# Gate matmuls of the second block's experts as fp32r halves, with GpSimd multiplying the low ones, and the choices of experts in another order

## The reference, cut to what matters

```python
def peer_ffn(h, peer_wq, peer_k1, peer_k2, peer_u, peer_v):
    q = (ht @ peer_wq).reshape(T, 8, 256)
    s1, s2 = q[..., :128] . peer_k1, q[..., 128:] . peer_k2        # T x 8 x 128 each
    v1, i1 = lax.top_k(s1, 16);  v2, i2 = lax.top_k(s2, 16)
    sc, pos = lax.top_k(v1[..., :, None] + v2[..., None, :], 16)   # best 16 of 256 pairs
    experts = i1[pos // 16] * 128 + i2[pos % 16]                   # T x 128 of 16384
    gates = softmax(sc)
    a = gelu(peer_u[experts] . h) * gates
    out = a @ peer_v[experts]
```

## Time and profile before

| what | value |
|---|---|
| time, three runs | median 2980.7 us (2978.4 to 2987.61) |
| the profiled execution | 2978.2 us |
| its span, first to last instruction | 2976.5 us |
| TensorE busy | 2824.8 us, 95% |
| VectorE busy | 2235.7 us, 75% |
| ScalarE busy | 1481.7 us, 50% |
| GpSimd busy | 582.0 us, 20% |
| mean granted clock of TensorE | 0.98 of full |

### The profile page before, as it was taken

How to read it: one execution, slowest core, us unless ns; L and a number is a source line. 1 busy time by engine, 2 the same in 40 slices (tenths; PEclk the granted TensorE clock), 3 DMA queues, 4 the chain that set the end, 5 groups by cost and what they waited for, 6 DMA issues and landing times.

```text
span 2976.5 us, 37320 instructions
## 1 busy us (share of the span) xinstructions
PE 2824.8 (95%) x13639; PEld 2359.7 (79%) x13639; DVE 2235.7 (75%) x3019; ACT 1481.7 (50%) x1990; POOL 582.0 (20%) x460
## 2 busy tenths in 40 slices
PE   5989987999999989999999999899999999999998
PEld 3666756888888857776777789899999998888887
DVE  6465546888888863696964599999777658888886
ACT  3433235888888843544552333555665633333332
POOL 0200111111111100000000000233333324444442
PEclk7999998999999999999999999999999999999999
DMA  7544635999999833232334324688998999999995
GB/s 305 171 160 146 212 137 205 368 372 367 363 360 352 324 140 128 86 114 89 117 106 149 114 86 142 236 293 308 322 319 310 326 337 358 368 364 357 362 371 174
DMA packets 201771, 737.90 MB, mean 248 GB/s; under 512 B 24432, under 2 KB 77808, under 8 KB 145008
## 3 DMA queue, kind: packets, MB, share of 16 engines
q1 hardware_dynamic: 124656, 497.12, 46.3%
q0 software_dynamic: 55056, 170.87, 16.7%
q10 hardware_dynamic: 21872, 67.48, 5.9%
HBM read 666.61 MB, written 93.91 MB: 256 GB/s over the span
## 4 chain that ended last, share of the span: by engine, by line
PE 64%; DVE 13%; issue 4%; ACT 2%; DMA 1%; ACTq 0%; DVEq 0%; SPq 0%; POOLq 0%
PE PS L544 55%; DVE wlo L1891 3%; PE PS L1145 2%; PE PS L1011 1%; PE PS L1023 1%; DVE hf L2700 1%; ACT whi L1221 1%; PE PS L850 1%; DVE oh L2674 1%; DVE hf L2688 1%; ACT HH L1861 1%; DVE cand L2640 1%; DVE cand L2642 1%; PE PS L1002 1%; DVE sS L2727 0%
## 5 line engine op out<-in xcount | busy, mean ns | idle before, releaser
L1891 DVE TENSOR_TENSOR wlo<-raw,whi 128x2048 fp32r<-128x2048 f32 x392 | 894.2, 2289 | 311.9 <-ACT whi L1221 270.9
L1221 ACT ACTIVATE whi<-raw 128x2048 fp32r<-128x2048 f32 x392 | 750.7, 1916 | 371.5 <-PE PS L544 317.3
L544 PE MATMUL PS<-HH,whi 128*128 128x512 f32 (+1 forms) x2056 | 787.8, 383 | 20.1 <-ACT HH L1257 10.1
L544 PE MATMUL PS<-HH,wlo 128*128 128x512 f32 (+1 forms) x2056 | 750.6, 365 | 0.0
L544 PE MATMUL PS<-HL,whi 128*128 128x512 f32 (+1 forms) x2056 | 750.3, 365 | 0.0
L544 PEld LDWEIGHTS PS<-HH,whi 128*128 128x128 f32 x2056 | 390.5, 190 | 78.1 <-issue 20.4
L544 PEld LDWEIGHTS PS<-HL,whi 128*128 128x128 f32 x2056 | 390.6, 190 | 46.6 <-issue 7.7
L544 PEld LDWEIGHTS PS<-HH,wlo 128*128 128x128 f32 x2056 | 389.3, 189 | 43.3
L544 PE MATMUL PS<-whi,HH 128*128 128x512 f32 (+1 forms) x896 | 350.6, 391 | 11.1 <-DVE HL L2730 5.8
L544 PE MATMUL PS<-whi,HL 128*128 128x512 f32 (+1 forms) x896 | 346.8, 387 | 0.0
L544 PE MATMUL PS<-wlo,HH 128*128 128x512 f32 (+1 forms) x896 | 346.8, 387 | 0.0
(11 more groups left out here) (434 smaller groups left out, 3891.9 us busy)
## 6 DMA issues: line engine op xcount, KB each, us to landing
raw<-in_moe_dram SPq DMA_DIRECT2D x192, 1024.0 KB, 7.2
raw<-in_u_units_dram SPq DMA_DIRECT2D x64, 1024.0 KB
raw<-in_v_units_dram SPq DMA_DIRECT2D x64, 1024.0 KB
raw<-in_w_in_dram SPq DMA_DIRECT2D x44, 1024.0 KB
raw<-in_w_ada_dram SPq DMA_DIRECT2D x24, 1024.0 KB, 20.1
acts_dram<-sS ACTq DMA_DIRECT2D x64, 384.0 KB
gates_dram<-XT ACTq DMA_DIRECT2D x24, 1024.0 KB
sS<-acts_dram SPq DMA_DIRECT2D x42, 384.0 KB
```

The costliest lines, as they stand in the source:

```text
L544: ins = t.matmul(dst, a, b, start=(first and n == 0), stop=(last and n == 2))
L1221: a.inc(a.e.activation(m.whi[p % HRING][:, :, :], m.raw[RAW_SLOT[load_of(p)]][:, :, :], ACT.Copy), "hi", p)
L1891: v.inc(v.e.tensor_tensor(m.wlo[h][:, :, :], m.raw[RAW_SLOT[load_of(p)]][:, :, :], m.whi[h][:, :, :].bitcast(F32), ALU.subtract), "lo_v", p)
```

## The change

Tile 0 is chosen first, so that gathered rows can start in chunk 13. A tile's exponential moves three chunks behind the end of its choice and behind that chunk's gate steps on ScalarE, and its sum, reciprocal and product (the share) four chunks behind, on VectorE. A gate matmul in fp32 becomes two in fp32r: one-hots are fp32r, the gates are split into a high part (ScalarE's copy into eT as fp32r) and the rest (`glow`, one VectorE instruction for a tile), ScalarE weights with the high part, and GpSimd multiplies the same one-hots with the low part into free corners of HH and HL (`gate_low`). ScalarE's weighting comes one step later, behind GpSimd. The planner counts 650 instead of 1100 for TensorE's gate step and may put two into one chunk, which it does in 16; by its arithmetic gate steps lie in chunks 33 to 119, tile 1 is chosen in chunks 12 to 28, tile 2 in 28 to 50 and tile 3 in 51 to 75. Semaphores follow.

```diff
-CHOICE_ORDER = (1, 0, 2, 3)
-CHOICE_NS = (1500, 4600, 4600, 2000, 3400, 3400, 3400, 3400, 800, 700)
+CHOICE_ORDER = (0, 1, 2, 3)
+CHOICE_NS = (1500, 4600, 4600, 2000, 3400, 3400, 3400, 3400, 800)
+EXP_AFTER, SHARE_AFTER, SHARE_NS = 3, 4, 700
...
-        row = ([], [], [])
+        row = ([], [], [], [i for i in chosen if n == chosen[i] + EXP_AFTER], [i for i in shared if n == shared[i]])
...
-            tensor += 1100
+            tensor += 650
...
-                self.oh = sb(s2, "oh", [128, 4, 2, 4, 128])
+                self.glow = sb(s2, "glow", [128, 2, 128])
+                self.oh = sb(s2, "oh", [128, 4, 2, 4, 128], F32R)
...
+def gate_low(m, n):
+    return (m.HH, m.HL)[n % 4 // 2][:, 4 * (n % 2):4 * (n % 2) + 4, 0:TD]
...
         for k in range(4):
-            ins = t.matmul(m.PS[:, 5 + n % 3, 128 * k:128 * k + 128], m.oh[:, n % 4, 0, k, :],
-                           m.oh[:, n % 4, 1, k, :], start=True, stop=True)
+            out = m.PS[:, 5 + n % 3, 128 * k:128 * k + 128]
+            t.matmul(out, m.oh[:, n % 4, 0, k, :], m.oh[:, n % 4, 1, k, :], start=True, stop=False)
+            ins = t.matmul(out, gate_low(m, n)[:, k, :], m.oh[:, n % 4, 1, k, :], start=False, stop=True)
...
-        a.inc(s.activation(m.eT[k % 2][:, 0:384], m.PS[:, 4, 0:384], ACT.Copy), "eT", i)
-    n = step - 3
+        a.inc(s.activation(m.eT[k % 2][:, 256:384].bitcast(F32R), m.PS[:, 4, 256:384], ACT.Copy), "eT_part", i)
+        a.inc(s.activation(m.eT[k % 2][:, 0:256], m.PS[:, 4, 0:256], ACT.Copy), "eT", i)
+    n = step - 4
     if 0 <= n < N_GATE:
         k, q = divmod(n, 32)
-        a.wait_ge("onehot", n)
+        a.wait_ge("lowered", n)
...
-        for step in PEER[n][0]:
-            act_choice_step(a, m, step)
         for step in PEER[n][1]:
             act_gate_step(a, m, step)
+        for i in PEER[n][3]:
+            act_choice_exp(a, m, i)
...
+        if q == 0:
+            if k > 1:
+                v.wait_ge("lowered", 32 * (k - 1) - 1)
+            v.inc(v.e.tensor_tensor(m.glow[:, k % 2, :], m.PS[:, 4, 256:384], eT[:, 256:384], ALU.subtract), "glow",
+                  TD // 128 + k)
+            v.own()
...
+        for i in PEER[n][4]:
+            dve_choice_share(v, m, i)
...
+def pool_gate_step(g, m, step):
+    n = step - 3
+    if 0 <= n < N_GATE:
+        k, q = divmod(n, 32)
+        g.wait_ge("glow", TD // 128 + k)
+        g.wait_ge("onehot", n)
+        g.inc(g.e.tensor_tensor(gate_low(m, n), m.oh[:, n % 4, 0, :, :].bitcast(F32),
+                                bass.AP(m.glow, 128 * (k % 2) + 4 * q, [[256, 128], [1, 4], [0, 128]]), ALU.mult),
+              "lowered", n)
...
     for n in range(128):
+        for step in PEER[n][1]:
+            pool_gate_step(g, m, step)
         for step in PEER[n][2]:
             pool_rows(g, m, step)
```

More of the change, by code:

```diff
@@ L174, in peer_schedule @@
 def peer_schedule():
-    up, chosen, a, b, c = [], {}, 0, 0, 0
+    up, chosen, shared, a, b, c = [], {}, {}, 0, 0, 0
     tensor, vector = 0, FOUND_NS
     for n in range(128):
-        row = ([], [], [])
+        row = ([], [], [], [i for i in chosen if n == chosen[i] + EXP_AFTER], [i for i in shared if n == shared[i]])
         tensor += 4200
         vector = max(vector, tensor - 4200) + 1150
-        first = chosen.get(TD // 128, n)
+        vector += SHARE_NS * len(row[4])
+        first = shared.get(TD // 128, n)
         while (b * (LAST_GATE - first) < GATE_STEPS * (n - first) and b < GATE_STEPS and len(row[1]) < 2
-               and (b >= N_GATE or n > chosen.get(TD // 128 + b // 32, n))):
+               and (b >= N_GATE or n > shared.get(TD // 128 + b // 32, n))):
             row[1].append(b)
             b += 1
-            tensor += 1100
+            tensor += 650
             vector += 1150
@@ L194, in peer_schedule @@
             i, r = choice_of(a)
-            if r == 0 and a and n == chosen[choice_of(a - 1)[0]]:
-                break
             row[0].append(a)
@@ L200, in peer_schedule @@
             if r == CHOICE_STEPS - 1:
-                chosen[i] = n
+                chosen[i], shared[i] = n, n + SHARE_AFTER
         up.append(row)
@@ L222 @@
     "peer_a": "xrow sq5 root5",
-    "choice": "top pick gsub gt index onehot",
+    "choice": "top pick gsub gt index glow onehot",
     "conv_a": "mean csq cdev zaff zact fstep",
@@ L1133, in pe_gate_step @@
         else:
-            pe.wait_ge("eT", i - 1)
+            pe.wait_ge("glow", i - 1)
         for k, src in enumerate((m.e1, m.e2, m.gt)):
@@ L1778, in act_scores, with act_choice_exp @@
     a.mark("scored")
[L1781 to L1786, removed]
+def act_choice_exp(a, m, i):
+    a.wait_ge("gsub", i)
+    dst = m.act0[:, :] if i * 128 < TD else m.gt[:, i, :, :].rearrange("p h k -> p (h k)")
+    a.inc(a.e.activation(dst, dst, ACT.Exp), "gexp5", i)
 def act_gate_step(a, m, step):
@@ L1810, in act_gate_step @@
             a.wait_ge("onehot", 32 * (k - 1) - 1)
-        a.inc(s.activation(m.eT[k % 2][:, 0:384], m.PS[:, 4, 0:384], ACT.Copy), "eT", i)
-    n = step - 3
+        a.inc(s.activation(m.eT[k % 2][:, 256:384].bitcast(F32R), m.PS[:, 4, 256:384], ACT.Copy), "eT_part", i)
+        a.inc(s.activation(m.eT[k % 2][:, 0:256], m.PS[:, 4, 0:256], ACT.Copy), "eT", i)
+    n = step - 4
     if 0 <= n < N_GATE:
         k, q = divmod(n, 32)
-        a.wait_ge("onehot", n)
-        a.wait_ge("eT", TD // 128 + k)
+        a.wait_ge("lowered", n)
+        a.wait_ge("eT_part", TD // 128 + k)
         for j in range(4):
             t = 256 + 4 * q + j
-            a.inc(s.activation(m.oh[:, n % 4, 0, j, :], m.oh[:, n % 4, 0, j, :], ACT.Copy,
+            a.inc(s.activation(m.oh[:, n % 4, 0, j, :], m.oh[:, n % 4, 0, j, :].bitcast(F32), ACT.Copy,
                                scale=m.eT[k % 2][:, t:t + 1]), "weighted_part" if j < 3 else "weighted", n)
@@ L2654, in dve_choice_step, with dve_choice_share @@
                               ALU.subtract), "gsub", i)
[L2655 to L2661, removed]
+def dve_choice_share(v, m, i):
+    e = v.e
+    dst = m.act0[:, :] if i * 128 < TD else m.gt[:, i, :, :].rearrange("p h k -> p (h k)")
+    G3 = dst.rearrange("p (h k) -> p h k", h=8)
+    v.wait_ge("gexp5", i)
+    v.inc(e.tensor_reduce(m.gs[:, :], G3, AX.X, ALU.add), "pick")
+    v.own()
+    v.inc(e.reciprocal(m.gs[:, :], m.gs[:, :]), "pick")
+    v.own()
+    v.inc(e.tensor_tensor(G3, G3, bass.AP(m.some, 16, [[32, 128], [1, 8], [0, 16]]), ALU.mult), "gt", i)
 def dve_gate_step(v, m, step):
```

## The result

The changed kernel took 2989.5 us (median of 20 runs, 2984.4 to 2995.3), the kernel before, run beside it, 2984.6 us (20 runs, 2978.4 to 2988.1). The ratio is 1.0022, with an interval of 1.0015 to 1.0028: 0.2% slower. The interval leaves zero out, but the difference is smaller than the 0.3% that the prediction took for no change. The forecast was 2985 on a before of 2980.7, that is +4; measured is +4.9.

What follows compares the result with a forecast made beforehand. TensorE was taken as the up stage's bound, VectorE close behind until chunk 60. Late exponentials -23, hold +28, others 0 gave +5 on 2978.2, 2983; with the shown median 2.5 higher, 2985, range 2957 to 3004.

Steps and rivals of the forecast that it cites:

- The exponentials and the order: Up stage: late exponentials remove three long TensorE waits and their slow clock, -23 us, if VectorE is in time elsewhere.
- The ledger: VectorE's work summed to chunk 72's end: 323 us, reaching 2128 like TensorE; without new GpSimd work VectorE keeps up.
- TensorE's share: Gate steps: eight fp32r matmuls at 0.112 take 0.90 us, as fp32 does; gain 0, bounds -40 and +5 us.
- Rival C: Gate matmuls in fp32r start 0.06 apart; only the 45 steps after chunk 78 gain: -15, 2970; chance 0.05.
- The hold: Chunks 37 to 78: GpSimd's multiplications cost VectorE 0.85 us each, 45 cost 38; less 10, TensorE waits 28 us.
- A: VectorE isn't held by GpSimd's multiplications (price 0): up stage ends at 2405, -23, time 2957; chance 0.18.
- D: Half of GpSimd's multiplications fall beside one-input instructions: 22 - 10 = 12, so -11, 2974; chance 0.06.
- The allowance: Up stage to chunk 72: how late VectorE may be before TensorE waits, taken as 10 us.
- rival B: GpSimd's multiplication between one-hot and weighting: hold costs 1.05 to 1.1 each, only 6 us allowed: +19, 3000; chance 0.28.
- The form of the loss: Up stage, from about chunk 37 to 78: TensorE loses 28 us in small pieces, many waits of 1 to 4 us.
- GpSimd's queue, 0 (up to 5): GpSimd's gathers and multiplications take 3.9 of 5.2 us a chunk: cost 0, up to 5 if gathers come late for dots.
- The signs to look for: Profile after: no copy-of-gates wait over 5 us, VectorE over 97%, its means up 0.2 to 0.4, GpSimd's 1.5 to 2.5.

Runs made afterwards that it cites:

- order_only: Changed kernel's new order, planner and late exponentials, but old fp32 gate matmuls and no GpSimd multiplications; against the kernel before: 2962.7 us, ratio 0.9934.
- defer_only: Kernel before with only exponentials three and shares four chunks later, old tile order, fp32 gate matmuls, no GpSimd multiplications: 2976.2 us, ratio 0.9969.
- the two narrow kernels: Changed kernel with gate matmuls moving only 64 of 128 columns, or loading only 64 of 128 weight columns: 2988.1 and 2968.1 us, single runs.
- write_only: Changed kernel with GpSimd's multiplication replaced by a memset that reads nothing, same waits and steps; against the kernel before: 2961.7 us, ratio 0.9933.
- narrow_moving: Changed kernel with gate matmuls moving only 64 of 128 columns, weights still 128 columns: 2988.1 us in a single run.
- pool_early: Changed kernel with each GpSimd multiplication one step earlier, ahead of that chunk's gathers; against the kernel before: 2988.5 us, ratio 1.0015.

## Why the prediction was right, point by point

**The exponentials and the order, -23.** order_only gives -21.4. In its starts of matmuls I find 16.5 us less of pauses over 0.3 us each, and some 5 less in steps stretched by less than that. The sum for the stage, 621, came out as 623.0. But the text gave the 23 to the deferral, "if VectorE is in time elsewhere", and defer_only shows that this condition was half of the gain: 9.9 by deferral, 11.5 by the order and the planning that goes with it. The ledger, which reckoned with the new order, was right that VectorE keeps up.

**TensorE's share, 0.** Right: a group is 0.896 and was 0.891 in order_only, 0.5 us in all, and the two narrow kernels bear out what the prediction read in the earlier trace rows. Rival C is out. The Trainium skill (TensorE: Matmul & The Clock Gate, LDWEIGHTS) has 107 ns for 128 columns loaded; the 0.112 of the changed kernel and of narrow_moving agrees. The same page's 81 ns for a sustained pair (Back-to-back issue gap) showed in no row of the gate matmuls.

**GpSimd's own time, 1.0.** Right: 1.033 at its shortest. The fixed part in it, which the prediction put at 0.1 without a row, comes to 0.18 by the two lengths (0.607 for 256 columns, 1.033 for 512). The Trainium skill (GPSIMD Engine Reference, §3), whose 4497 ns for 2048 columns I had turned into an estimate of 1.1 to 1.2, lay a little above.

**The hold, +28.** The mechanism is shown: no loss with a GpSimd that only writes, 11.5 us at half the reading, 26.4 at all of it. Rivals A and D are out; of 49 multiplications seven stood beside one-input instructions or searches, not half. (D's time was also reckoned from the wrong start: -11 on 2980.7 is 2970, not 2974.) The size was right by luck, because two terms were off against each other.

The price was 0.85 each, and the forecast's own band for it began at 0.7. It is 0.64 in VectorE's busy time. In the stretch from 1930 to 2180, where it matters, each VectorE instruction's time over the shortest of its form, summed, is 33 us more than in write_only, for 49 multiplications: 0.67. How often one holds was about right, 0.92 x 0.92 = 0.85 against 39 of 49. How long wasn't: the sum took the multiplication's whole length, 1.0, and the trace has 0.84 to 0.90 at the most, 0.48 to 0.72 in ten cases, 0.81 in the mean of the 39.

The allowance was 10 us. In the prediction's own count, by VectorE's low half of chunk 73 and 46 multiplications, the hold is 29.7 us more than in write_only, and TensorE ends that chunk, counted from the stage's start, 26.5 us later than there. So 3 us were left of the 10, less even than rival B's 6: 38 - 10 = 28 stands against 29.7 - 3.2 = 26.5. Two chunks before, the allowance was as forecast: TensorE ended chunk 71 17.5 us later than in write_only and VectorE's low half started 27.7 later, so VectorE was 10.2 us further behind. The long wait at 2147.5 and the slow clock behind it then took 9 us of TensorE's time.

**The form of the loss.** Wrong in part. The text had TensorE lose it in small waits of 1 to 4 us and named no clock. Against write_only the 26.4 us are 18.1 in pauses over 0.3 us and 7.9 in steps stretched by less; 7.1 us of these stand from 1980 to 2010, 2050 to 2060 and 2150 to 2160, where the granted clock is low. One wait was 6.5, with a clock of 0.58 for 5.8 us behind it. The term that was missing is the clock's answer to new waits, 7 to 8 us; it is part of the 26.4 and of what shrank the allowance above.

**GpSimd's queue, 0 (up to 5).** Right in the time: pool_early changes the stage by 0.3 us. That is a net figure, since VectorE is busy 3.9 us longer there (2302.1 against 2298.2). A gather in front of the multiplication does lengthen single waits.

**The signs to look for.** No wait of TensorE over 5 us on the copies of gates: so. VectorE over 97% up to 2150: 98.3% from 1930 to 2150. The low half's mean 0.2 to 0.4 above 2.29: it is 0.46 above, one-hots 0.20 and 0.24, dots only 0.07 to 0.13. GpSimd's mean 1.5 to 2.5: 1.49. What a group lost goes by how often it came next behind a multiplication, which the equal marks left out: from 1930 to 2420 33 of 46 low halves were longer than their shortest by over 0.06 us, 29 of 96 one-hots and 12 of 99 dots.

**The sum.** -23 + 28 + 0 = +5 stands against -21.4 + 27.2 = +5.8 in the stage of the profiled executions, and +4.9 in the medians.

What stays open: why a pick step is held for less (0.65 to 0.72) than a one-hot of the same length (0.84), whether the hold goes by the elements that GpSimd reads or by the length of its reading instruction, and how much of order_only's gain is the order of the tiles and how much the planner's.

## What to carry to other kernels

A change that moves work to an idle engine and one that reorders work can each be worth 20 us and cancel; sum them apart, and run them apart, or a gain of 0.7% (order_only) lies hidden in a result of no change. When a helper engine reads SBUF beside an engine that is 96% busy with two-operand instructions, charge the busy engine for the helper's reading instructions, 0.5 to 0.6 us for each us of them here, before asking whether the helper has time. And where a queue is unblocked by a deferral, ask what is late next: half of the gain hung on an order and a plan in which nothing was.

## What the runs showed of the hardware

- GpSimd's time and its hold on VectorE were equal for the same number of elements read: copying 512 columns and multiplying 256 by 256 took 0.612 and 0.607 us and cost VectorE 0.28 each; multiplying 512 by 512 took 1.033 and cost 0.64; writing 512 took 0.524 and cost nothing that can be seen.
- A multiplication of GpSimd that started within a two-input instruction of VectorE ended 0.90 us behind its end (43 of 49), and VectorE's next two-input instruction was mostly 0.84 to 0.90 us longer (29 of 49). A one-input reduction (L2651) kept its 1.22 us.
- A GpSimd instruction of 128 columns took 0.59 us, hardly less than one of 512 read once. Cutting in four made 96 instructions' work cost 115 us of stage (765.6 against 650.2).
- fp32r matmuls of 128 columns with new weights each followed each other by 0.112 us, also with 64 moving columns, and by 0.06 with 64 weight columns. One fp32 matmul cost as much as two of fp32r, so a high and a low half gained nothing, and the high half alone gained 32 us of stage (591.1 against 623.0).
